# Decays of two kinds of heads from running sums instead of TensorE products, and a rope without rotation products, in a two-block model on one core

## What is computed

```python
# fox: attention with a forget gate
log_f = log_sigmoid(f_raw + b_f); F = cumsum(log_f)            # per head, over 256 tokens
s = q @ k.T * 64 ** -0.5 + F[q] - F[k]                          # masked to k <= q
# ssm: 16 heads, chunks of 64, equal to one causal product over all 256 tokens
dt = softplus(dt_raw + dt_bias); a_cum = cumsum(dt * A)         # A = -exp(A_log)
y = sum_j (C_i . B_j) * exp(a_cum_i - a_cum_j) * dt_j * x_j + D * x_i     # j <= i
# mla: rope on 32 of 96 entries of q and k, after a norm over the 96
rot = concat([x1 * cos - x2 * sin, x1 * sin + x2 * cos])
```

## Time and profile before

| | us |
|---|---|
| median of 3 runs | 1173.43 (1172.96 to 1176.35) |
| the profiled run, whole | 1176.22 |
| its span | 1174.4 |
| prologue, to the first fox score | 134 |
| fox heads | 71 |
| mla heads | 55 |
| ssd heads, to the end of the last values | 90 |
| first FFN and all behind it | 824 |

### The profile page before, as it was taken

One profiled execution on the slowest core, in us unless ns is written; L12 is line 12 of the kernel. 1 busy time (PEld: TensorE's weight loads), 2 busy tenths in 40 slices (PEclk: granted clock), 3 DMA queues, 4 the chain that ended last, 5 costly groups with the idle time before them and its releaser, 6 DMA issues.

```text
span 1174.4 us, 21776 instructions
## 1 busy us (share of the span) xinstructions
PE 1152.0 (98%) x8784; PEld 1082.2 (92%) x8784; DVE 778.9 (66%) x1227; ACT 599.5 (51%) x946; POOL 103.6 (9%) x112
## 2 busy tenths in 40 slices
PE   8999999999999999999998999999999999999997
PEld 8986788889999999999996999999999879999997
DVE  6864587665767799995664577775655446777653
ACT  6663555653465666654432444435567645444453
POOL 0010122004530033330000000000000000000000
PEclk9999999999999999999998999999999999999999
DMA  9332333333434555535641555535653115455451
GB/s 354 133 142 99 153 108 126 109 108 126 181 143 146 183 195 194 194 128 183 230 140 63 189 196 192 184 124 189 226 180 109 72 72 215 179 182 180 144 187 62
DMA packets 30077, 185.54 MB, mean 158 GB/s; under 512 B 3472, under 2 KB 3728, under 8 KB 13104
## 3 DMA queue, kind: packets, MB, share of 16 engines
q1 hardware_dynamic: 29424, 183.40, 44.0%
q10 hardware_dynamic: 576, 1.05, 0.3%
HBM read 183.39 MB, written 1.05 MB: 157 GB/s over the span
## 4 chain that ended last, share of the span: by engine, by line
PE 90%; DVE 6%; ACT 3%; issue 1%; DMA 1%; SPq 0%; DVEq 0%; ACTq 0%
PE bank L852 71%; PE bank L900 6%; DVE w_lo L1734 2%; PE bank L909 1%; PE O L1230 1%; PE S L1132 1%; ACT w_hi L1323 1%; PE T L1203 1%; PE bank L934 1%; ACT pr L1559 1%; PE S L833 1%; PE bank L944 1%; PE S L1260 1%; PE bank L833 1%; DMA x<-x_in 1%
## 5 line engine op out<-in xcount | busy, mean ns | idle before, releaser
L1323 ACT ACTIVATE w_hi<-ring 128x1024 fp32r<-128x1024 f32 (+2 forms) x348 | 316.3, 957 | 338.9 <-PE bank L852 338.7
L1734 DVE TENSOR_TENSOR w_lo<-ring,w_hi 128x1024 fp32r<-128x1024 f32 (+2 forms) x348 | 370.4, 1106 | 154.3 <-ACT w_hi L1323 153.0
L852 PE MATMUL bank<-xh,w_hi 128*128 128x256 f32 x1600 | 454.1, 284 | 0.3 <-DVE w_lo L1734 0.3
L852 PE MATMUL bank<-xh,w_lo 128*128 128x256 f32 x1600 | 449.1, 281 | 0.0
L852 PE MATMUL bank<-xl,w_hi 128*128 128x256 f32 x1600 | 449.0, 281 | 0.0
L852 PEld LDWEIGHTS bank<-xh,w_hi 128*128 128x128 f32 x1600 | 301.7, 189 | 2.8 <-issue 1.8
L852 PEld LDWEIGHTS bank<-xl,w_hi 128*128 128x128 f32 x1600 | 301.8, 189 | 0.2
L852 PEld LDWEIGHTS bank<-xh,w_lo 128*128 128x128 f32 x1600 | 301.5, 188 | 0.0
L852 PE MATMUL bank<-hid_hi,w_hi 128*128 128x256 f32 x528 | 148.4, 281 | 0.6 <-DVE w_lo L1734 0.6
L852 PE MATMUL bank<-hid_lo,w_hi 128*128 128x256 f32 x528 | 148.3, 281 | 0.0
L852 PE MATMUL bank<-hid_hi,w_lo 128*128 128x256 f32 x528 | 148.3, 281 | 0.0
(11 more groups left out here) (301 smaller groups left out, 1671.1 us busy)
## 6 DMA issues: line engine op xcount, KB each, us to landing
ring<-w_up SPq DMA_DIRECT2D x22, 1024.0 KB, 4.7
ring<-w_upa SPq DMA_DIRECT2D x22, 1024.0 KB, 4.8
ring<-w_upb SPq DMA_DIRECT2D x22, 1024.0 KB, 4.8
ring<-w_gate SPq DMA_DIRECT2D x12, 1024.0 KB, 4.9
ring<-w_down SPq DMA_DIRECT2D x16, 704.0 KB, 4.0
ring<-w_downa SPq DMA_DIRECT2D x16, 704.0 KB, 4.1
ring<-w_downb SPq DMA_DIRECT2D x16, 704.0 KB, 4.1
ring<-w_xbc SPq DMA_DIRECT2D x6, 1024.0 KB, 4.8
```

The source lines that it names most:

```text
L852: last = mm(out, lhs, rhs, start=(start and k == 0 and (a, b) == (0, 0)), **kw, stop=(whole and k == ks[-1] and (a, b) == (1, 0)))
L1323: A(w_hi[:, q % 2, a:e], raw[:, a:e], ACT.Copy).then_inc(hi_ready, 1)
L1734: last = V.tensor_tensor(w_lo[:, q % 2, a:e], raw[:, a:e], w_hi[:, q % 2, a:e], ALU.subtract)
```

## The change

- The running sums are made once, for all 24 heads. A new step `cs`, right behind `ft`, does six small products on TensorE: rows of F and a_cum (24 x 256) and columns of a_cum. ScalarE copies the rows to SBUF and the columns to `sums`.
- SyncE writes the rows to DRAM (`rows`), and then reads each head's row back to all 128 partitions (`row`), into tiles that are free by then. It waits for each tile to be free ahead of the transfer.
- GpSimd makes the decay of a fox head by adding the row to the mask; VectorE then takes `G` in place of the mask (the part of F that is constant along a row falls out in the softmax). For ssd it adds the column and takes the minimum with 0 in three operations, and ScalarE takes the exp from `G`. TensorE does nothing for it: fox scores are two products, ssd scores none.
- The rope: the weights give a second, swapped copy of the 32 entries, so 128 entries on 128 partitions. It is then one product with a table of cosines and sines. The keys' common part is made once (`kt`, then a product `kf` of 256 columns). Angles are worked out once on 64 partitions instead of twice on 32. The norm sums and the q products become 128 wide.
- `uk` takes two groups instead of four, and its products write the two halves of a bank in turn.
- The dense groups are xbc 0, z 0, xbc 1, z 1, xbc 2, z 2, xbc 3, z 3, xbc 4, xbc 5; the rest is as it was.

```diff
-    st += [("nm", "f1"), ("ft",), ("trig", 2)]
-
-    st += [("g", "uq", 2), ("nm", "m0"), ("sq", "f2"), ("sq", "m1"), ("g", "uq", 3), ("g", "fv", 0), ("trig", 3)]
+    st += [("nm", "f1"), ("ft",), ("cs",)]
+
+    st += [("g", "uq", 2), ("nm", "m0"), ("sq", "f2"), ("sq", "m1"), ("g", "uq", 3), ("g", "fv", 0)]
     st += [("nm", "f2"), ("nm", "m1"), ("sq", "f3"), ("sq", "m2"), ("sin",), ("g", "fv", 1), ("nm", "f3")]
-    st += [("rope", 0), ("sq", "m3"), ("g", "memkv", 0), ("nm", "m2"), ("rope", 1)]
-    st += [("g", "uk", 0), ("nm", "m3"), ("g", "uk", 1), ("sq", "m4"), ("g", "uk", 2), ("g", "uk", 3), ("rope", 2)]
-    st += [("nm", "m4"), ("sq", "m5"), ("g", "uv", 0), ("g", "uv", 1), ("rope", 3)]
+    st += [("kt",), ("rope", 0), ("sq", "m3"), ("g", "memkv", 0), ("nm", "m2"), ("kf",), ("rope", 1)]
+    st += [("g", "uk", 0), ("nm", "m3"), ("g", "uk", 1), ("sq", "m4"), ("rope", 2)]
+    st += [("nm", "m4"), ("sq", "m5"), ("rows",), ("g", "uv", 0), ("g", "uv", 1), ("rope", 3)]
     for t in range(5, 8):
-        st += [("g", "memkv", t - 4), ("rope", t - 1), ("nm", f"m{t}")] + ([("sq", f"m{t + 1}")] if t < 7 else [])
+        st += [("row", "fox", 2 * t - 10), ("row", "fox", 2 * t - 9), ("g", "memkv", t - 4), ("nm", f"m{t}")] + ([("sq", f"m{t + 1}")] if t < 7 else [])
 
...
-    dense = [("g", "xbc", n) for n in range(6)] + [("g", "z", n) for n in range(4)]
+    dense = [("g", stage, n) for n in range(4) for stage in ("xbc", "z")] + [("g", "xbc", 4), ("g", "xbc", 5)]
...
+    ROWS = {14: (0, 1), 15: (2, 3), 18: (4, 5), 19: (6, 7), 21: (8, 9), 23: (10, 11), 25: (12, 13), 26: (14, 15)}
...
-        out = dense[t:t + 1] + ([] if t else [("rope", 7)])
+        out = dense[t:t + 1]
...
+        out += [("row", "fox", h) for h in (6, 7) if t == 0] + [("row", "ssd", h) for h in ROWS.get(t, ())]
...
+        def row_of(k, h):
+
+            if k == "fox":
+                return merged[:, h, :]
+            if h < 12:
+                return mqk[:, h if h < 8 else 4 + h, :]
+            return flat(mv)[:, (h - 12) * S:(h - 11) * S]
+
+        def row_here(k, h):
+
+            return row_in[h % 8], 16 if k == "fox" else 32 + 16 * (h // 8)
 
...
+                elif s[0] == "rows":
+                    sp.wait_ge(rows_ready, 1)
+                    sp.dma_start(rows_d[:, :], rows).then_inc(rows_out, 16)
+                elif s[0] == "row":
+                    _, k, h = s
+                    if (k, h) == ("fox", 0):
+                        sp.wait_ge(rows_out, 16)
+                    if k == "ssd" and h < 12:
+                        sp.wait_ge(s_done, S_USE["A", "mla", h if h < 8 else h - 4] + 1)
+                    elif k == "ssd":
+                        sp.wait_ge(o_done, 2 * FOX_H)
+                    line = h if k == "fox" else FOX_H + h
+                    sp.dma_start(row_of(k, h), rows_d[line:line + 1, :].partition_broadcast(P))\
+                        .then_inc(row_here(k, h)[0], 16)
...
-                    last = feature_major(stage, i, W, 2, DM, [(2 * i * P, NOPE, 0), ((2 * i + 1) * P, NOPE, 0)],
-                                         lambda k: cqkv[:, 3 + k, :], after("ckv") if i == 0 else None)
+                    if i == 0:
+                        pe.wait_ge(normed, NORMED["ckv"] + 2)
+                    b = banks[g % RING]
+                    for m in range(2):
+                        for k in range(2):
+                            for odd in range(2):
+                                o = k * DM + (4 * i + 2 * m + odd) * P
+                                last = mm(b[64 * odd:64 * odd + 64, m * S:m * S + S], W[:, o:o + NOPE],
...
                 _, k, h = s
+                if k == "ssd":
+                    return
                 b = s_bank(s)
-                if k == "ssd":
-                    n["decay"] += 1
-                    pe.wait_ge(decay_ready, n["decay"])
-                    H = G[:, h % 2, :]
-                    mm(b[:, 0:S], H[:, 0:P], C("le_ones"), start=True, stop=False)
-                    mm(b[:, P:S], H[:, P:2 * P], C("le_ones", 0, P), start=False, stop=True)
-                    mm(b[:, S:384], H[:, 2 * P:384], C("le_ones", 0, P), start=True, stop=True)\
-                        .then_inc(s_done, 1)
-                    return
                 q, key, _, _ = head_io(k, h)
                 if k == "fox":
                     if h == 0:
                         pe.wait_ge(normed, NORMED["f3"] + 1)
...
-                    n["decay"] += 1
-                    pe.wait_ge(decay_ready, n["decay"])
-                    g = G[:, h % 2, :]
-                    mm(b[:, 0:P], q[:, 0:P], key[:, 0:P], start=True, stop=False)
-                    mm(b[:, 0:P], C("le8_ones8", 0, P), g[:, 0:P], start=False, stop=True)
-                    mm(b[:, P:384], q[:, P:S], key, start=True, stop=False)
-                    mm(b[:, P:S], C("le8_ones8", P, S), g[:, 0:P], start=False, stop=False)
-                    mm(b[:, P:384], C("le8_ones8", 0, P), g[:, P:384], start=False, stop=True)\
-                        .then_inc(s_done, 1)
+                    mm(b[:, 0:P], q[:, 0:P], key[:, 0:P], start=True, stop=True)
+                    mm(b[:, P:384], q[:, P:S], key, start=True, stop=True).then_inc(s_done, 1)
                 elif k == "mla":
                     if h == 0:
-                        pe.wait_ge(roped, 8)
...
+                elif s[0] == "cs":
+                    b = t_bank(s)
+                    pe.wait_ge(f_ready, 1)
+                    le, ones = C("le_ones", 0, P), C("ones")
+                    more = dict(start=False, stop=False, skip_group_check=True)
+                    v0, v1 = steps[:, 0, FOX_H:24], steps[:, 1, FOX_H:24]
+                    mm(b[:, S:S + SSM_H], le, v0, start=True, stop=False, skip_group_check=True)
+                    mm(b[:, S + SSM_H:S + 2 * SSM_H], le, v1, **more)
+                    mm(b[:, S + 2 * SSM_H:S + 3 * SSM_H], C("gt"), v0, **more)
+                    mm(b[0:24, 0:P], steps[:, 0, :], le, **more)
+                    mm(b[0:24, P:S], steps[:, 1, :], le, **more)
+                    mm(b[0:FOX_H, P:S], steps[:, 0, 0:FOX_H], ones, start=False, stop=True, skip_group_check=True)\
+                        .then_inc(t_done, 1)
...
-                    act.wait_ge(s_done, u + 1)
+                    act.wait_ge(decay_ready, FOX_H + h + 1)
                     if n["weights"] >= 2:
                         act.wait_ge(weighted, n["weights"] - 1)
                     n["weights"] += 1
-                    A(pr[:, r, 0:384], b[:, 0:384], ACT.Exp, bias=C("zero")).then_inc(s_free[u % 2], 1)
-                elif k == "sb":
+                    A(pr[:, r, 0:384], G[:, r, 0:384], ACT.Exp, bias=C("zero")).then_inc(decayed, 1)
...
+                elif s[0] == "cs":
+                    act.wait_ge(t_done, T_USE[s] + 1)
+                    A(rows, Tb[0:24, 0:S], ACT.Copy).then_inc(rows_ready, 1)
+                    A(sums[:, 0:32], Tb[:, S:S + 32], ACT.Identity, bias=C("zero"), scale=-1.0)
+                    A(sums[:, 32:48], Tb[:, S + 32:S + 48], ACT.Copy).then_inc(t_free, 1)
...
+                        if k == "fox":
+                            dve.wait_ge(decay_ready, h + 1)
                         stt(sc[:, r, 0:384], b[:, 0:384], SC64 if k == "fox" else SC_MLA,
-                            C("m_fox" if k == "fox" else "m_mla"), ALU.mult, ALU.add).then_inc(s_free[u % 2], 1)
+                            G[:, r, 0:384] if k == "fox" else C("m_mla"), ALU.mult, ALU.add).then_inc(s_free[u % 2], 1)
...
+                elif s[0] == "kt":
+                    dve.wait_ge(trig_ready, 1)
+                    stt(kt[NOPE:P, :], mqk[NOPE:P, 8, :], Pm("mla_k_gain", 0, NOPE, P), trig[NOPE:P, 0, :],
+                        ALU.mult, ALU.mult).then_inc(kt_ready, 1)
+                elif s[0] == "kf":
+                    u = S_USE[s]
+                    dve.wait_ge(s_done, u + 1)
+                    V.tensor_copy(kf[NOPE:P, :], Sb[u % 2][NOPE:P, 0:S]).then_inc(s_free[u % 2], 1)
                 elif s[0] == "rope":
                     i = s[1]
-                    u = S_USE[s]
-                    dve.wait_ge(s_done, u + 1)
-                    dve.wait_ge(trig_ready, 1)
-                    rows = slice(NOPE, QK)
-                    part = flat(mqk[rows, 2 * i:2 * i + 2, :])
-                    if i:
-                        dve.wait_ge(roped, i)
-                    stt(tg[rows, 0, :], Sb[u % 2][rows, :], 1.0, trig[rows, 0, :], ALU.mult, ALU.mult)\
-                        .then_inc(s_free[u % 2], 1)
-                    own(V.tensor_tensor(part, part, trig[rows, 1, :], ALU.mult))
-                    dve.wait_ge(s_free[u % 2], u // 2 + 1)
-                    V.tensor_tensor(part, part, tg[rows, 0, :], ALU.add).then_inc(roped, 1)
+                    dve.wait_ge(normed, NORMED[f"m{i}"] + 1)
+                    part = mqk[NOPE:P, 2 * i:2 * i + 2, :]
+                    V.tensor_tensor(part, part, trig[NOPE:P, :, :], ALU.mult).then_inc(roped, 1)
...
```

(27 more changed lines are left out.)

148 lines of the change are left out of this document (83 added, 65 removed).

## The result

| | before | changed |
|---|---|---|
| median, us | 1173.20 (1171.61 to 1176.35, 4 runs) | 1160.95 (1159.63 to 1163.13, 4 runs) |
| profiled run, us | 1176.22 (span 1174.4) | 1159.63 (span 1157.8) |
| ratio to before | | 0.9891, 95% interval 0.9874 to 0.9909 |

The account below looks back on a forecast made before the run. TensorE and VectorE were taken as level, so VectorE and loops through both hold the ticks. Prologue -1.9, fox and mla +3.0, ssd +3.8 give 4.9 us won of 38.6 counted: 1171.3 profiled, 1168.5 as median, range 1157 to 1177.

Parts of the forecast that it names:

- Prologue: Before the heads: stall, cs, clock and kf outweigh fewer rotations and cheaper uk; 1.9 us lost, between 6 lost and 2 won.
- The stall: Behind the ft transposes, TensorE idles until cs gets the last softplus result, with later groups queued behind; 7.5 us.
- the 1.3 + 2.8 of the sum: Prologue: 1.3 us for the cs products plus 2.8 us lost to TensorE's lowered clock after the idle stretch.
- the longer products after them: Prologue: part of the 7.6 us saved by removing seven rotations together with the products following them.
- Fox and mla: Fox and mla heads: pairs fall from 17.75 to 16.3 us, part given back in later ticks; 3.0 us won, bounds 0 and 6.
- rival C: Fox ticks: the turn's waits lower TensorE's clock, up to 4.6 us each; three give 1177 to 1182; chance 0.13.
- Ssd: Ssd heads: values still wait for VectorE's weighted scores, so removing TensorE's scores wins only 3.8 us, between 1 and 7.
- the full 4.8 of the count: Ssd heads: gain from pairs, first pair and last ticks, before 1.0 us is taken off for GpSimd beside VectorE.
- New here: Ssd heads: GpSimd's decay operations coincide with VectorE's weighted scores and slow them; half of 0.48 us per waiting pair, 1.0 lost.
- Rival B: Ssd and fox heads: GpSimd takes VectorE's time in all pairs, about 3 us more; 1171.5 us, chance 0.21.
- In the FFN and behind it nothing is changed.: FFN and everything after it: no term was put in the sum for this part of the kernel.
- Rival A: Whole kernel: TensorE's count holds, 25.7 us won, 1147.7 us; a part gives 1150 to 1163; chance 0.13 with its parts.

Follow-up runs that it names:

- old places: Changed kernel with an unused block and the sums ahead of x, so x, xh, xl and all behind lie at their earlier addresses; 1169.55 us, ratio 0.9967.
- the 64 bytes: Changed kernel with 64 unused bytes behind sg, moving the upper memory up while x, xh and xl stay; 1156.97 us, ratio 0.9864.
- cs_later: Changed kernel with the six cs products moved from directly behind ft to behind fv 0; 1152.31 us, ratio 0.9820.
- both: Changed kernel with cs behind fv 0 and 64 unused bytes ahead of the upper-memory tensors; 1149.77 us, ratio 0.9790.
- old_order: Kernel with the 64 bytes, dense groups beside the heads in the old order, all six xbc then four z; 1157.02 us.

## Why the prediction was right and where it was wrong

The changed kernel at the old places has the old pitch, so it is this one that the steps of the sum are held against. Starts in us, from TensorE's timelines:

```
                      before   old places   changed
ft transposes          61.71      60.87      60.60
first fox score       133.70     134.65     134.58
first mla score       204.66     199.11     198.72
last turn of mla      262.16     261.10     260.49
first brs product     349.72     345.50     343.08
first FFN, up         404.8      400.3      398.0
end of the span      1174.4     1167.3     1157.8
```

**Prologue**: forecast 1.9 lost. The changed program reaches `ft` 0.84 earlier, which I haven't followed up; from there to the first fox score it needs 73.78 instead of 71.99 us, 1.8 lost. The stall is 7.55 as forecast. `cs` with the fallen clock is 2.77 and the first uq group 1.48 longer than before: 4.25 against the 1.3 + 2.8 of the sum. `kf` takes 0.57, forecast 0.8; the wait for m4's squares is 0.35, forecast 0.5. The pairs of uk products do run side by side, 16 instructions in 1.9 us:

```profile
100.96 0.64 PE L1288 MATMUL S<-xbc,cst 64*64 64x256 f32 x2
101.54 1.95 PE L1054 MATMUL bank<-xbc,ring 128*64 128x256 f32 x16
```

The second group takes 1.9 as well (the wait for m4's squares comes behind it), together 3.8 where the four took 7.2 in the kernel before: 3.4 saved, forecast 3.5. That leaves 7.5 for the rotations and all else in the prologue, forecast 7.6; of the forecast only the 6.8 of seven rotations stand in a row, for the 0.8 of "the longer products after them" it gives no working. The row transfers cost nothing: only GpSimd waits for them, and nobody waited more than 0.2 us for its decays.

**Fox and mla**: forecast 3.0 won, measured 2.0 (2.01 from first fox score to last turn). A fox score is 0.85 us (157.12 to 157.97 in the changed kernel), forecast 0.84; a pair is 16.2 (157.12 to 173.31), forecast 16.3; then 4.5 are given back, forecast 4.3. The fall of the clock in the fox heads, rival C, is in it with 1.6; without it 3.6 would have been won. The window where it happened in the changed kernel, then the same window with the 64 bytes:

```profile
184.00:188.00 4.00, 4.00 (x23) 4.00 (x22) 3.59 (x6) 2.33 (x6) 0.00 (x0) 0.57 0.29 53
...
184.00:188.00 4.00, 4.00 (x37) 4.00 (x36) 2.91 (x7) 2.25 (x7) 0.00 (x0) 1.00 0.35 118
```

Behind the same wait of 1.44 us the clock fell in one profile and not in the other. In the heads it fell once in the changed kernel's profile, twice at the old places and in cs_later, and three times in `both` and old_order. A fall costs 1.6 us (a pair of 17.77 instead of 16.19), not the 4.6 that I took from the pool stage: the clock is back at full in 188 to 192, while there it was low for some 9 us. Rival C's mechanism is real and its price a third of mine; three falls, the most that a profile here has in the heads, cost 4.8 us at that price, and no kernel here came out slower than the one before for it.

**Ssd**: forecast 3.8, measured 3.2 (87.56 us from the last turn to brs, 84.40). The pair went from 11.24 to 11.12, forecast 11.12; the stretch from the last regular pair to the last values from 30.04 to 26.69 (3.35, forecast 3.4). The first pair, from the last turn to its values, took 11.78 us before and 10.82 in the changed kernel, so the forecast 0.9 came; at the old places it took 12.42, as the clock fell behind the 2.1 us wait of the last turn:

```profile
262.00:266.00 4.00, 4.00 (x23) 4.00 (x23) 1.62 (x4) 0.73 (x2) 2.34 (x3) 0.57 0.63 195
```

Without this fall, 1.6, the ssd heads would have won the full 4.8 of the count. What the forecast took off them, 1.0 for GpSimd, didn't happen. GpSimd in the kernel before, then VectorE and GpSimd in the changed one:

```profile
282.20 2.71 POOL L2239 TENSOR_SCALAR G<-cst,adt 128x256 f32<-128x256 f32 x1
...
281.50 0.78 DVE L2085 SCALAR_TENSOR_TENSOR sc<-pr,fdt,cbm 128x256 f32<-128x256 f32 x2
282.20 1.28 DVE L1780 TENSOR_TENSOR w_lo<-ring,w_hi 128x512 fp32r<-128x512 f32 x2
...
281.53 0.95 POOL L2301 TENSOR_SCALAR G<-mqk,sums 128x128 f32<-128x128 f32 x1 [5.42 <-ACT pr L1576]
...
275.40 0.71 POOL L2303 TENSOR_SCALAR G<-mqk,sums 128x128 f32<-128x128 f32 x1
```

The prediction's "New here" was a misreading: the 0.88 of the earlier trace rows was itself measured with GpSimd at work (282.20 to 284.91). Alone the operation takes 0.74, so in the changed kernel it loses 0.04, and not the 0.24 that went into the sum. GpSimd's own operation gets longer, 0.95 instead of the 0.71 of the last line, but nobody waits for it. Rival B didn't happen here. By the rule of the Trainium skill's "SBUF — State Buffer", section "🔬 SBUF: two separate sides", whichever of the two starts first has the port for the whole instruction. At 281.50 that agrees, for VectorE comes first and GpSimd is lengthened. In the pair's other head it doesn't:

```profile
285.80 0.77 DVE L2085 SCALAR_TENSOR_TENSOR sc<-pr,fdt,cbm 128x256 f32<-128x256 f32 x2
...
285.43 0.95 POOL L2302 TENSOR_SCALAR G<-mqk,sums 128x128 f32<-128x128 f32 x1
```

GpSimd comes first there, and is again the one that is lengthened. The measurement decides as to VectorE's time; why the FFN's taps do get longer beside GpSimd (0.47 alone, up to 0.98) and these scores don't is open.

In all 4.2 us by the traces up to the end of ssd and 3.9 by the ratio of the runs, against 4.9. That the two are so near is partly luck: two falls of the clock, 3.2 us, aren't in the sum, and against them stand 1.0 for GpSimd, 0.6 in the fox and mla heads and the 0.84 by which `ft` is reached earlier. Behind it the two differ by 2.9 us more, 2.4 of it between the first FFN's last down product and the products on mixa (50.9 and 48.5 us), where the profiled run of the kernel before had a granted clock of 0.90 and the others 0.97. The prediction took 2.8 off its profiled run for just such a difference.

**The step that failed** is the sentence "In the FFN and behind it nothing is changed." No instruction is, but the addresses are, and with 7488 dense matmuls a pitch of 2 ns less would be 15 us if all of them had it. From the FFN's start to the end the changed kernel takes 759.8 us and the one at the old places 767.0. The forecast put this term at nothing; the runs show 8.4 of the 12.3 us there, and in the dense groups beside the heads. The diff says it (three constants go or shrink), and the trace of before can't price it, for it shows one place only; a range for it would have been honest. Rival A, whose parts reached over the measured time, is not what happened: VectorE holds the ticks as forecast.

## What to carry to other kernels

A count of what leaves the busiest engine is an upper bound. Write down the loop through all engines; the removed work is worth what is left when the next one is late. A changed order can earn some of what the removal didn't: the waiting product behind half a dense group won about 3 us at the ssd values, and lost more than that at the turns where another product needed the same bank.

When a change resizes any tensor, ask what moves behind it. Compare two versions at equal addresses before their difference is ascribed to the edit; and try a block of 64 or 128 unused bytes ahead of the operands of a long row of matmuls, which costs only memory and gave 0.8% to the kernel before.

A product that needs a late result of another engine belongs behind independent groups, not where its inputs are drawn up. The stall was plain in the trace of before and cost 8.6 us with the clock.

## What the runs showed of the hardware

- Back-to-back fp32r matmuls of 256 columns, weight loads between them, at the full clock: 116.7 to 121.1 ns from start to start, by where the stationary and the moving operand lie in the partition. The Trainium skill, "TensorE: Matmul & The Clock Gate", section "Wait — 56ns, not 53.3ns?", gives columns over 2.4 GHz and about 2.5 ns more for back-to-back matmuls, which by an estimate is 109.2 ns for 256 columns; no stretch here reaches that.
- The clock stayed at full for the first 2 us of the idle stretch, was at the lower level from 66 to 74, though TensorE was dense again from 68.45 on, and was back at 1.00 in 76:78. In the heads' ticks a wait of 1.4 to 2 us brought it down in some executions and not in others, for about 1.6 us of time each where no other engine held the tick.
- VectorE's weighted scores and GpSimd's decay beside each other in the changed kernel: 0.78 us instead of 0.74, and 0.95 instead of 0.71.
- Products of 64 columns of weights into different halves of a bank's partitions run side by side: 16 in 1.9 us, where 8 took as long before.
